# Opening a fused decoder kernel by token groups: the second group's v half, o, out and second query run after the gathers have begun

## The reference, cut to what matters

```python
def _peer(xn, wq, subkeys, u, v):              # for a chunk of 128 tokens
    q = (xc @ wq).reshape(T, PEER_HEADS, 2, PEER_HALF)
    s = jnp.einsum('thpd,pkd->thpk', q, subkeys)
    s_top, i_top = lax.top_k(s, K)             # then the best 16 of 16 x 16 sums: idx, best_s
    act = gelu(einsum('thkd,td->thk', u[idx], xc))
    return einsum('thk,thkd->td', softmax(best_s) * act, v[idx])

# layer 0, before its PEER; mod = silu(c) @ ada_w + ada_b, six pieces of 1024
xn = _ada_rmsnorm(x, mix_norm, sh1, sc1)
q, k, v, o = split(xn @ w_in)                  # mLSTM over chunks gives h
x = x + g1 * ((sigmoid(o) * head_rms(h)) @ w_out)
xn = _ada_rmsnorm(x, ffn_norm, sh2, sc2)       # what PEER's query and its dots read
```

## Time and profile before

| | |
|---|---|
| median of three runs | 1787.74 us (1785.43 to 1788.91) |
| the profiled execution | 1785.12 us |
| its span, first to last instruction | 1783.0 us |
| busy: PE, DVE, ACT, POOL | 86%, 58%, 21%, 60% |
| granted TensorE clock, mean | 0.973 of full speed |
| moved by DMA | 682.92 MB, mean 383 GB/s |

### The profile page before, as it was taken

One profiled execution on the slowest core, in us unless ns is written; L12 is line 12 of the kernel. 1 busy time (PEld: TensorE's weight loads), 2 busy tenths in 40 slices (PEclk: granted clock), 3 DMA queues, 4 the chain that ended last, 5 costly groups with the idle time before them and its releaser, 6 DMA issues.

```text
span 1783.0 us, 13512 instructions
## 1 busy us (share of the span) xinstructions
PE 1524.6 (86%) x3952; PEld 662.9 (37%) x3952; DVE 1029.9 (58%) x2479; ACT 381.8 (21%) x959; POOL 1068.3 (60%) x1131
## 2 busy tenths in 40 slices
PE   4997949999898878999997777999999777777777
PEld 3754424443232323444442223444443222222223
DVE  6547772686665653255377774336449885444542
ACT  2121222221111122142121113133222212111110
POOL 4212366767565674446467775447547777777773
PEclk9998969999999999999999998999999999999999
DMA  9997479999999999999999999999999999999996
GB/s 374 399 367 256 148 274 404 398 405 404 405 405 405 407 409 384 383 375 404 402 405 409 409 409 406 367 390 409 402 361 406 409 408 405 409 410 409 410 409 270
DMA packets 212573, 682.92 MB, mean 383 GB/s; under 512 B 20851, under 2 KB 21525, under 8 KB 212502
## 3 DMA queue, kind: packets, MB, share of 16 engines
q0 software_dynamic: 158976, 578.88, 82.6%
q1 hardware_dynamic: 52464, 101.79, 15.3%
q10 hardware_dynamic: 1062, 1.40, 0.2%
HBM read 680.94 MB, written 1.05 MB: 383 GB/s over the span
## 4 chain that ended last, share of the span: by engine, by line
PE 42%; DMA 29%; POOL 17%; issue 6%; DVE 5%; ACT 1%; POOLq 0%; DVEq 0%
PE pair L990 19%; PE pair L181 15%; DMA net_u<-in_peer_u,net_cols 11%; DMA net_v<-in_peer_v,net_cols 10%; POOL net_v L564 8%; POOL net_u L564 8%; DMA net_w<-in_b_w_qo 2%; DMA net_w<-in_peer_wq 2%; DVE net_u L1748 2%; PE pair L194 2%; PE pair L201 1%; DMA net_v<-in_ada_w 1%; DMA net_w<-in_kv_w 1%; PE pair L592 1%; PE pair L731 1%
## 5 line engine op out<-in xcount | busy, mean ns | idle before, releaser
L990 PE MATMUL pair<-net_v,net_diags 128*128 128x512 f32 x2048 | 977.2, 611 | 158.3 <-DMA net_v<-in_peer_v,net_cols 158.0
L564 POOL DMA_INDIRECT net_v<-in_peer_v,net_cols x512 | 500.8, 978 | 338.2 <-PE pair L990 216.1
L990 PEld LDWEIGHTS pair<-net_v,net_diags 128*128 128x128 f32 x2048 | 367.1, 191 | 715.9 <-DMA net_v<-in_peer_v,net_cols 362.3
L564 POOL DMA_INDIRECT net_u<-in_peer_u,net_cols x512 | 505.2, 987 | 210.7 <-issue 133.0
L1748 DVE SCALAR_TENSOR_TENSOR net_u<-net_u,pair 128x1024 f32<-128x1024 f32 x384 | 464.1, 1217 | 254.7 <-DMA net_u<-in_peer_u,net_cols 254.3
L181 PE MATMUL pair<-net_w,net_work 128*128 128x512 f32 x640 | 300.8, 616 | 37.7 <-DMA net_w<-in_b_w_qo 16.3
L1332 ACT ACTIVATE net_diags<-ident,net_cols 128x128 f32<-128x128 f32 x512 | 170.9, 390 | 685.1 <-DVE net_cols L1428 685.1
L1748 DVE SCALAR_TENSOR_TENSOR net_u<-net_u,net_x_tok 128x1024 f32<-128x1024 f32 x128 | 156.3, 1222 | 110.8 <-DMA net_u<-in_peer_u,net_cols 110.4
L181 PEld LDWEIGHTS pair<-net_w,net_work 128*128 128x128 f32 x640 | 124.4, 198 | 189.8 <-issue 173.0
L223 POOL DMA_DIRECT2D net_u<-in_ada_w x46 | 24.8, 543 | 80.9 <-DVE net_cols L235 20.1
L1428 DVE TENSOR_TENSOR net_cols<-net_cols,net_gate 128x4 f32<-128x4 f32 (+1 forms) x124 | 19.7, 159 | 92.0 <-ACT net_cols L1325 91.9
(11 more groups left out here) (242 smaller groups left out, 958.9 us busy)
## 6 DMA issues: line engine op xcount, KB each, us to landing
net_w<-in_peer_wq SPq DMA_DIRECT2D x12, 2048.0 KB, 19.8
net_u<-in_ada_w POOLq DMA_DIRECT2D x46, 512.0 KB, 8.3
net_w<-in_ada_w SPq DMA_DIRECT2D x8, 2048.0 KB, 19.9
net_w<-in_kv_w SPq DMA_DIRECT2D x8, 2048.0 KB, 18.0
net_w<-in_b_w_qo SPq DMA_DIRECT2D x8, 2048.0 KB, 18.9
net_v<-in_ada_w POOLq DMA_DIRECT2D x18, 512.0 KB, 12.7
net_u<-in_kv_ada_w POOLq DMA_DIRECT2D x16, 512.0 KB, 4.8
net_u<-in_peer_u,net_cols POOLq DMA_INDIRECT x512, 11.5
```

Of the source, the lines that this page charges most:

```text
L564: eng.indirect_dma_start(slot, None, rows, bass.IndirectOffsetOnAxis(ap=idx[:, i, k:k + 1], axis=0)).then_inc(landed, 16)
L990: mm = eng.matmul(acc[q % 2][:, at], diag[n % DIAGS][:, :], vb[n % V_SLOTS][:, at], start=(k == 0), stop=(k == SEL - 1))
```

## The change

Group 0 of the opening is done first, and most of group 1 after group 0's first query:

- PE's order after `key_scores(0)` was: row for the gate, column sums, o0, sums, o1 of group 0, `key_scores(1)`, out0, out1 of group 0, `sums(1)`, o0 of group 1, query 0, o1 of group 1, query 1, out0, out1 of group 1. It becomes: o0, sums, o1 of group 0, row, `key_scores(1)`, out0, out1 of group 0, column sums, half of v1 of group 1, query 0, the other half, o1 of group 1, query 1, `sums(1)`, o0b, out0b, out1 of group 1.
- o0b and out0b are the blocks o0 and out0 loaded a second time, into slot 1: 2 x 2048 KB more. wq0 moves to slot 4 and wq1 to slot 3, and with them every later block changes between 3 and 4.
- DVE's adds of the modulation are split otherwise between its other work. `add_mix(0)` follows piece 63 (before: piece 71). The last five adds follow `route(0)`. `mlstm_scale(1)` and `mlstm_y(1)` move into the loop, behind steps 3 and 7, `add_mix(1)` from behind step 10 to behind step 14, the evacuation of group 1 from 15 to 25.
- POOL no longer waits for all adds before the first gather. It issues gathers 0 to 3, then the load of piece 79, and then waits for all 80 adds. `mlstm_root(1)` moves to its step 12, `norm_root(3)` from step 13 to 26. The buffer order of pieces 48 to 79 is turned by two.
- `QUERY_AT`, `ROW_AT`, `VEC_AT` move later by 11 to 12 steps (by 8 to 11 for r = 5 to 7), `VEC_EVERY` goes from 9 to 8, `NEAR_AT` from 32 to 48.

```diff
     EDGES = list(range(0, PER, 2 * BATCH)) + list(range(PER, N + 1, BATCH))
-    NEAR_AT = 32
+    NEAR_AT = 48
...
-                  "o0": (wi, 2 * qk_cols + v_cols, GROUP, 4), "o1": (wi, 2 * qk_cols + v_cols + WCOLS, GROUP, 0),
-                  "out0": (a["a_w_out"][0], 0, GROUP, 1), "out1": (a["a_w_out"][0], WCOLS, GROUP, 2)}
-        wide = [f"wq{n}" for n in range(4)] + [f"vec{n}" for n in range(8)]
-        for n in range(4):
-            blocks[f"wq{n}"] = (a["peer_wq"][0], n * WCOLS, GROUP, 3 + n % 2)
+                  "o0": (wi, o_cols, GROUP, 4), "o1": (wi, o_cols + WCOLS, GROUP, 0),
+                  "out0": (wo, 0, GROUP, 1), "out1": (wo, WCOLS, GROUP, 2),
+                  "wq0": (a["peer_wq"][0], 0, GROUP, 4), "o0b": (wi, o_cols, GROUP, 1),
+                  "wq1": (a["peer_wq"][0], WCOLS, GROUP, 3), "out0b": (wo, 0, GROUP, 1)}
+        wide = ["wq2", "wq3"] + [f"vec{n}" for n in range(8)]
+        for n in range(2, 4):
...
-                     ada_slots, [n if n < 16 else (4, 5, 6, 7, 16, 17)[(n - 16) % 6] if n < 48 else 4 + n % 4
+                     ada_slots, [n if n < 16 else (4, 5, 6, 7, 16, 17)[(n - 16) % 6] if n < 48 else (6, 7, 4, 5)[n % 4]
...
-        QUERY_AT = {2: 1, 3: 3, 4: 6, 5: 12, 6: 18, 7: 24}
-        ROW_AT, VEC_AT, VEC_EVERY = 34, 40, 9
+        QUERY_AT = {2: 12, 3: 14, 4: 17, 5: 22, 6: 27, 7: 32}
+        ROW_AT, VEC_AT, VEC_EVERY = 46, 52, 8
...
-            for name in ("v0", "v1", "o0", "o1", "out0", "out1"):
+            for name in ("v0", "v1", "o0", "o1", "out0", "out1", "wq0"):
...
-            for name in wide:
+            for name in ["o0b", "wq1", "out0b"] + wide:
                 pj.load(eng, name)
...
-            ada.load(eng, 16, 38)
+            ada.load(eng, 16, 37)
             mlstm_root(0)
-            ada.load(eng, 54, 22)
+            ada.load(eng, 53, 15)
             norm_root(2)
-            ada.load(eng, 76, 4)
-            mlstm_root(1)
+            ada.load(eng, 68, 11)
 
             def roots():
-                yield 4 - 13
+                yield 12 - POOL_SHIFT
+                mlstm_root(1)
+                yield 26 - POOL_SHIFT
                 norm_root(3)
                 for g in range(G):
...
             eng.wait_ge(pj.done, pj.through("o1", 1))
-            eng.wait_ge(ada.added, ADA)
             for n in range(N + LAG):
                 if n < N:
                     if n % PER == 0:
                         eng.wait_ge(idx_done, n // PER + 1)
                     if n >= U_SLOTS:
                         eng.wait_ge(dot_done, n - U_SLOTS + 1)
+                    if n == 4:
+                        ada.load(eng, ADA - 1, 1)
+                        eng.wait_ge(ada.added, ADA)
                     behind.upto(n)
                     gather(u_rows, n, ub[n % U_SLOTS], u_in[n % U_SLOTS])
...
-            eng.wait_ge(ml_evac, 1)
-            pj.whole(eng, "v1", 1, bank[4], Dw)
...
             key_scores(0, bank[5], (bank[0],))
-            eng.wait_ge(ml_evac, 6)
+            pj.whole(eng, "o0", 0, bank[1], C)
+            eng.wait_ge(ml_evac, 7)
+            eng.wait_ge(arg_done, 1)
+            sums(0, pair[2])
+            pj.whole(eng, "o1", 0, bank[6], C)
...
             mm.then_inc(row_ps, 1)
+            eng.wait_ge(y_ready, 1)
+            turn(pair[2], A).then_inc(ml_turned, 1)
+            eng.wait_ge(so_done0, 2)
+            key_scores(1, bank[0], (bank[1], bank[6]))
+            eng.wait_ge(row_copied, 1)
+            eng.wait_ge(ml_yT, 1)
+            pj.whole(eng, "out0", 0, bank[2], E)
+            pj.whole(eng, "out1", 0, bank[3], E)
             eng.wait_ge(cols_done, 2)
             column_sums(cols, DC, DC, AUX[:, 2 * DC:3 * DC])
-            pj.whole(eng, "o0", 0, bank[1], C)
-            eng.wait_ge(ml_evac, 8)
-            eng.wait_ge(arg_done, 1)
-            sums(0, pair[2])
-            pj.whole(eng, "o1", 0, bank[6], C)
-            eng.wait_ge(row_copied, 1)
-            eng.wait_ge(so_done0, 1)
-            key_scores(1, bank[0], (bank[1], bank[2]))
-            eng.wait_ge(y_ready, 1)
-            turn(pair[2], A).then_inc(ml_turned, 1)
             eng.wait_ge(ada.added, 5 * DC)
             column_sums(sc0, 0, DC, AUX[:, 3 * DC:4 * DC])
-            eng.wait_ge(ml_yT, 1)
             eng.wait_ge(sd_done, 3)
-            pj.whole(eng, "out0", 0, bank[2], E)
-            pj.whole(eng, "out1", 0, bank[3], E)
-            eng.wait_ge(pw_done, 3)
-            sums(1, pair[0])
-            eng.wait_ge(x_mix, 1)
-            pj.part(eng, "o0", 1, bank[2], Dw, 0)
+            pj.part(eng, "v1", 1, bank[0], Dw, 0)
             eng.wait_ge(xs_done, 3)
             turn(pair[2], A).then_inc(x_turned, 1)
-            pj.part(eng, "o0", 1, bank[2], Dw, 1)
...
             query(0, "wq0", C, 1)
             turn_query(0)
             score_keys(0)
-            pj.whole(eng, "o1", 1, bank[3], Dw)
+            pj.part(eng, "v1", 1, bank[0], Dw, 1)
             eng.wait_ge(sc_done, 1)
             turn_tokens(0, 0)
-            eng.wait_ge(hmean, 2)
+            pj.whole(eng, "o1", 1, bank[2], Dw)
             query(1, "wq1", C, 0)
             query(1, "wq1", C, 1)
             eng.wait_ge(copied, 1)
             turn_query(1)
+            eng.wait_ge(pw_done, 3)
+            eng.wait_ge(ml_evac, 8)
+            sums(1, pair[0])
+            score_keys(1)
+            pj.whole(eng, "o0b", 1, bank[3], Dw)
             eng.wait_ge(y_ready, 2)
             turn(pair[0], B).then_inc(ml_turned, 1)
-            score_keys(1)
-            eng.wait_ge(ml_yT, 2)
-            eng.wait_ge(so_done0, 4)
-            pj.whole(eng, "out0", 1, bank[2], F)
-            pj.whole(eng, "out1", 1, bank[3], F)
             eng.wait_ge(sc_done, 2)
             eng.wait_ge(ada.added, 6 * DC)
             column_sums(sc0, DC, DC, bank[5][:, 0:DC])
-            eng.wait_ge(xs_done, 4)
-            turn(pair[1], B).then_inc(x_turned, 1)
+            eng.wait_ge(ml_yT, 2)
+            eng.wait_ge(so_done0, 4)
+            pj.whole(eng, "out0b", 1, bank[2], F)
+            pj.whole(eng, "out1", 1, bank[3], F)
 
...
                     g, j = FIRST[r]
+                    if r == 2:
+                        yield QUERY_AT[2] - 3
+                        eng.wait_ge(xs_done, 4)
+                        turn(pair[1], B).then_inc(x_turned, 1)
...
             eng.wait_ge(pj.done, pj.through("o1", 0))
             eng.activation(so[0][:, WCOLS:2 * WCOLS], bank[6][:, :], ACT.Sigmoid).then_inc(so_done0, 1)
-            eng.wait_ge(ml_rows, 2)
-            for h in range(ML_H):
-                done = eng.activation(pw[1][:, h * P:(h + 1) * P], bank[0][:, h * P:(h + 1) * P], ACT.Exp,
-                                      bias=acol[:, 0, h:h + 1], scale=-1.0)
-            done.then_inc(pw_done, 1)
+            eng.wait_ge(row_ps, 1)
+            eng.activation(row_mix[:, :], pair[1][:, :], ACT.Copy).then_inc(row_copied, 1)
 
             def take_y(g, src, dst):
                 eng.wait_ge(ml_turned, g + 1)
@@ -1097,6 +1104,11 @@
                 done.then_inc(ml_yT, 1)
 
             take_y(0, pair[2], E)
+            eng.wait_ge(ml_rows, 2)
+            for h in range(ML_H):
+                done = eng.activation(pw[1][:, h * P:(h + 1) * P], bank[0][:, h * P:(h + 1) * P], ACT.Exp,
+                                      bias=acol[:, 0, h:h + 1], scale=-1.0)
+            done.then_inc(pw_done, 1)
             eng.wait_ge(arg_done, 2)
...
                 if r >= 2:
                     eng.wait_ge(q_turned, r - 1)
-                eng.activation((Dw if r else F)[:, half:half + 512], bank[6 + r % 2][:, :], ACT.Copy).then_inc(q_copied, 1)
+                eng.activation((F if r < 2 else Dw)[:, half:half + 512], query_bank(r)[:, :], ACT.Copy).then_inc(q_copied, 1)
...
+            take_values("v1", 1, WCOLS, bank[0])
+            copy_tokens(0, 0)
             eng.wait_ge(pj.done, pj.through("o1", 1))
...
             copy_query(1, "wq1", 0)
             copy_turned(1)
+            exponent(0)
+            head_squares(1, pair[0])
+            copy_scores(1, sc[0], 1)
+            eng.wait_ge(pj.done, pj.through("o0b", 1))
+            eng.activation(so[1][:, 0:WCOLS], bank[3][:, :], ACT.Sigmoid).then_inc(so_done0, 1)
             take_y(1, pair[0], F)
-            copy_scores(1, sc[0], 1)
-            exponent(0)
 
...
                 eng.activation(acc[(q + 1) % 2][:, :], x_tok[:, :], ACT.Copy).then_inc(tok_near, 1)
 
             def first_queries():
-                yield -5
+                yield QUERY_AT[2] - 13
                 eng.wait_ge(x_mix, 2)
                 square(3, 1)
-                yield -4
+                yield QUERY_AT[2] - 6
                 scale(3, 1)
...
+            ada.add(eng, 44, 5)
             mlstm_scale(0)
+            ada.add(eng, 49, 4)
             mlstm_y(0, pair[2])
+            ada.add(eng, 53, 1)
             eng.wait_ge(pw_done, 2)
             masked(2, pw[2], bank[0])
             weighed(1, 2, bank[1])
```

(40 more changed lines are left out.)

## The result

The changed kernel takes 1804.52 us (median of 6 runs, 1801.71 to 1812.73), the kernel before beside it 1788.33 us: a ratio of 1.010, 95% interval 1.0079 to 1.0121. It is 16 us slower; the forecast was 1784.2, the range 1775 to 1796. Its profiled execution has a span of 1800.1 us against 1783.0.

The account below looks back on a forecast made before the run. It took DMA at some 404 GB/s as the bound after an opening with 46.7 us of idle DMA; -3.9 (opening) + 0.4 (query burst) = -3.5 against 1785.1 profiled gave 1781.6, plus 2.6 for the median: 1784.2, range 1775 to 1796.

Parts of the forecast that it names:

- The opening up to the first dot: Opening through first gathers: first gather at 182.6 us (206.25 before), first dot at 194.3 behind piece 79, 16.5 us earlier.
- the two extra blocks are hidden: Opening: o0b and out0b, 5.2 us each at 404 GB/s, cost nothing because they load while DMA has idle time.
- The gate: End of opening, before v0: y_ready at 213.7 us, out1 of group 1 ends at 234.7 (222.0 before), v0 at 235.1.
- cost nothing: Opening, PE after query 0: v1's second half and o1 end near 178.5 us, before route(0), with 3.5 us to spare.
- the term of -3.9: End of opening: gather u13 goes out at 236.4 us instead of 240.30, so the kernel ends 3.9 us earlier.
- the v gate gives all of it back: Rival, opening: the gather loop starts earlier but gains nothing at the v gate; -2 to +3 us, 1788, chance 0.14.
- The yardstick u13: End of opening: the kernel's end moves as much as gather u13 (240.30 us before), from which gathers run without a gap.
- The query burst: Loop, queries 2 to 7: r = 4 scored near 333 us, DVE waits from near 315; 0.4 us lost, bounds 0 to 5.
- 10.4 of queued blocks and some 3 in flight: Loop, near 321 to 334 us: queued blocks and gathers in flight keep DMA busy while POOL stands 13 us.
- Query 2 starts when step 26's batch is through ACT: Loop, start of the queries: query 2 begins near 281 us (255.52 before).
- query 2 comes late: Rival, loop: each us after 281 holds DVE longer at step 38, deciding from about 284; +5 to +12, about 1795, chance 0.17.
- The lock: Rival, loop rounds: 16 more steps each with gathers slowed by the port lock VectorE and GpSimd share; +4 to +10, chance 0.04.

Follow-up runs that it names:

- Experiment 6: Changed kernel with norm_root(3) and queries 2 to 4 earlier, v gate in two, group 1's mlstm_scale, root and y ahead of route(1): ratio 0.9944 to the kernel before.
- the later companies: Four later sets of follow-up kernels, each on one chip beside the kernel before (1862 to 1876 us); the changed kernel's ratio was 1.0014 in one, 1.0062 in another.
- experiment 2: Changed kernel with norm_root(3) at step 19, queries 2 to 7 at steps 9 to 31, transpose and evacuations earlier: ratio 1.0041 to the kernel before.
- Experiments 1 to 3: Kernel before with only the changed loop timetable, 1.0094; changed kernel with norm_root(3) and all queries earlier, 1.0041; the same with queries 5 to 7 put back, 0.9974.
- experiment 8: NEAR_AT alone: changed kernel with 32, ratios 1.0074 and 1.0051 (1.0062 with 48 beside the latter); kernel before with 48, 1.0000.

## Why the prediction was wrong

**The opening up to the first dot: right.** out1 of group 0 ended at 138.3 (136.8 foretold), `add_mix(0)` began at 145.59 (145.3), the first gather left at 182.92 (182.6), piece 79 made POOL stand 7.41 us and the first dot began at 195.87 (194.3; the terms add up to 194.2). That the two extra blocks are hidden held too: they moved in windows that had room, 369 GB/s for 211 in 120 to 140 us and 326 for 183 in 200 to 220, and PE waited for neither. Experiment 6 shows where it would stop.

**The gate: mechanism right, terms small.** The row of L1504 below is `mlstm_y(1)`; y was ready at 216.8, 213.7 foretold. 1.6 us of that were lost by the first dot, the rest by a wait that the sum did not have: DVE stood 2.37 us at the first piece of `route(1)` for the scores of query 1. v1's second half and o1 do not "cost nothing": wq1 goes into slot 3, so it could not be loaded before v1's last half was multiplied (170.6), PE waited 2.97 us for it, and the product behind that wait took 8.83 us for 7.0, the first half of it near half clock (granted clock 0.66 in 182 to 184 us, 0.50 in 184 to 186, 0.99 in 186 to 188). In the later companies' traces of the changed kernel the scores came before DVE read them, so this wait is not in every execution. Behind y the sum held: out0b and out1 took 16.50 us, 16 foretold, and out1 ended at 238.4 (234.7), u13 left at 239.95 (236.4). So the term of -3.9 became -0.35, which is the rival "the v gate gives all of it back".

```profile
181.33 8.83 PE L181 MATMUL pair<-net_w,net_work 128*128 128x512 f32 x16 [2.97 <-DMA net_w<-in_peer_wq]
...
200.61 0.87 DVE L1358 MAX8 net_top<-net_sc 128x8 f32<-128x128 f32 x4 [2.37 <-ACT net_sc L1140]
...
215.18 1.66 DVE L1504 SCALAR_TENSOR_TENSOR net_work<-pair,net_rr,net_v 128x256 f32<-128x256 f32 x4
...
216.89 1.97 PE L602 MATMUL pair<-ident,net_work 128*128 128x128 f32 x8 [8.84 <-DVE net_work L1504]
218.65 3.41 PE L607 MATMUL pair<-ones,net_sc 128*128 128x1 f32 x16
221.93 16.50 PE L181 MATMUL pair<-net_v,net_work 128*128 128x512 f32 x32
```

The yardstick u13 held as well. At 240 us POOL's queue had moved 0.53 MB less than in the kernel before, which had sent v0 at 228.16, before `norm_root(3)`:

```profile
228.16 1.08 POOL L564 DMA_INDIRECT net_v<-in_peer_v,net_cols  x1 [0.30 <-issue]
```

But the changed kernel sent v0 too before u13 (238.70), and at 260 us its queue was 0.06 MB ahead. The 1.4 us that the windows show at 340 us were lost later, in 260 to 300 us: 378 and 382 GB/s for 394 and 403. There POOL issued without a pause in both kernels (30 and 29 gathers), and SP's queue filled up the rest in the kernel before with 4.09 MB of blocks, in the changed one with 0.11, since its query blocks could not come before query 2.

**The query burst: this step failed.** The prediction let POOL stand 13 us and set "10.4 of queued blocks and some 3 in flight" against it: 0.4 us lost. POOL stood less, 8.37 us, and still 7.7 us of DMA were idle at once, 9.6 with the windows behind it. The cover was not there. Of the DMA queues, q0 is POOL's with the gathers and q1 is SP's with the blocks. In the changed kernel q1 moved both blocks in 300 to 340 us, beside gathers and before POOL stood; in 340 to 370 us q1 moved nothing:

```profile
q1 hardware_dynamic: 2026, 4.08, 26.9%
...
q0 software_dynamic: 2427, 8.84, 80.5%
```

(packets, MB, share of 16 engines; the first row is 300 to 340 us, the second 340 to 370.) The gathers in flight kept DMA full for some 6 us after POOL's last one (2.04 MB in 340 to 345 us, 0.23 in the five behind), and then it stood. The reading that the cover came from was wrong already in the kernel before: POOL stood 7.66 us in the earlier trace rows, but q1 moved 0.11 MB in the 30 us around it, and the 4.10 MB of 302 to 312 us were all gathers in flight.

```profile
q1 hardware_dynamic: 68, 0.11, 1.0%
```

The wait itself was mis-sized too. DVE waited 25.15 us, from 320.6 to 345.8, where the sum has 315 to 334. "Query 2 starts when step 26's batch is through ACT" was right, but it started at 286.89 and not near 281; 3.6 us of that are the late gate. Between a query's product and its scores PE waited 5.37 us for ACT, so query 4 was scored 57 us after query 2 began, for 51 in the kernel before. And DVE's wait was priced by the reading of the scores, when ACT's list sets it at `weigh`, in front of that reading: the gelu behind all the copies of the queries before it. In the changed kernel the two nearly coincide (345.57 behind 345.08), in experiment 2 they are 13 us apart. Experiments 1 to 3 show the last two. The rival "query 2 comes late" was the right one, with +5 to +12 and a chance of 0.17; by its own rule (1 us for each us after 284) it gives 3 for 286.89, and 7.7 came.

**The lock: not shown as a cost.** In the late stretch of the first trace the stretching is plain. DVE's dots with tokens in SBUF and POOL's gathers beside them, changed kernel:

```profile
1501.79 1.23 DVE L1762 SCALAR_TENSOR_TENSOR net_u<-net_u,net_x_tok 128x1024 f32<-128x1024 f32 x1 [1.45 <-DMA net_u<-in_peer_u,net_cols]
1502.70 1.13 POOL L572 DMA_INDIRECT net_v<-in_peer_v,net_cols  x1 [0.30 <-PE pair L999]
...
1504.67 1.23 DVE L1762 SCALAR_TENSOR_TENSOR net_u<-net_u,net_x_tok 128x1024 f32<-128x1024 f32 x1 [1.65 <-DMA net_u<-in_peer_u,net_cols]
1505.39 1.33 POOL L572 DMA_INDIRECT net_v<-in_peer_v,net_cols  x1 [0.30 <-PE pair L999]
```

A gather that begins while such a dot runs ends 0.81 or 0.82 us after the dot's end (1503.83 for 1503.02, 1506.72 for 1505.90), one that begins without it takes 0.94. The rows agree with what the Trainium skill, "SBUF — State Buffer", section "SBUF: two separate sides", says of an exclusive lock on the port pair that the two engines share. In this stretch POOL never waits, 0.30 us between gathers, so here its stretched gathers hold DMA back. But experiment 8 finds no difference between 16 more such dots in each round and none, so that NEAR_AT is the reason is not shown. So some 9 of the 17 us, those of 1440 to 1580, stay open: they are in the one trace of 1800 us, the six times around 1804.5 suggest that they were there each time, and in the later companies they could not be told from what all kernels show. That the same change is worth 1.010 in one company and 1.001 in another fits this, and is not an explanation.

## What to carry to other kernels

When a loop is bound by DMA, an opening is worth only what it brings forward of the point from which transfers run without a gap, and that is checked in bytes moved, window by window; look first for who stands in front of that point, here a single root in POOL's list. Work that is moved from the opening into the loop sits in the in-order lists of four engines: for each piece, ask what is behind it in its own list, and what waits for that. Here a gelu behind the copies of a query stopped DVE (in experiment 2 for 13 us after the scores were there), and then POOL, and then DMA. A stand of the issuing engine is covered only by what is still queued at that hour: look up in the trace which queue moves what during such a stand before you count on it. And a wait that seems to set a start (piece 79) can have the next one close behind it: take it away in thought and name the next wait before counting it.

## What the runs showed of the hardware that was not expected

POOL issues a u and a v gather in 2.48 us (0.94 each and 0.30 between them), and DMA takes 2.56 to 2.6 us for their megabyte. So there is hardly anything in hand: a gather stretched to 1.33 us leaves POOL slower than DMA, and the changed kernel's window of 1480 to 1500 us shows that, with PE idle for over a quarter of the time and DVE for half:

```profile
1480.00:1500.00 20.00, 14.31 (x27) 4.55 (x25) 9.92 (x19) 5.76 (x13) 15.91 (x14) 0.91 0.98 363
```

And the kernel before took 1788 us beside the changed one at first and 1862 to 1876 us in the later companies. It has no trace in those companies, but its variant with NEAR_AT 48 has: on the plateau (slices 10 to 15) nothing tells the two apart, 404 to 409 GB/s in both; what was lost lies behind it. On all four chips of the later companies the kernel before took that longer, and whether the chip or the hour makes the later part slower, the runs don't show.
